# Gate projections as seven half-size products: weight sums on GpSimd, result sums on VectorE

## The reference

```
def trunk_layer(x, ple, pos, lp, lb, cache):
    proj = x @ lp['w_in']
    cq, ckv, kr, f_pre, q_pre, i_pre, g_pre, ga, gb = jnp.split(proj, ...)
    ...
    merged = jax.nn.sigmoid(ga) * (a @ lp['w_br_a']) + jax.nn.sigmoid(gb) * (o @ lp['w_br_b'])
    x = layernorm(DN_ALPHA * x + merged @ lp['w_out'], lp['ln1_g'], lp['ln1_b'])
    moe_out = hier_moe(x, ...)
    ...
```

## Time and profile before

| | us |
|---|---|
| median of 3 runs (lowest, highest) | 1529.96 (1529.62, 1530.68) |
| profiled execution, first to last instruction (span) | 1528.1 |
| PE busy | 1285.5 (84%) |
| PEld busy | 723.5 (47%) |
| DVE busy | 403.9 (26%) |
| ACT busy | 284.9 (19%) |
| POOL busy | 54.0 (4%) |

### The profile page before, as it was taken

The page is one execution under the profiler, slowest core; times in us unless marked ns, Lnnn a source line. Parts: engine busy times, 40 slices in busy tenths (PEclk is TensorE's granted clock), DMA queues, the critical chain, the costliest instruction groups (busy, mean ns, idle before and its releaser), DMA issues.

```text
span 1528.1 us, 20304 instructions
## 1 busy us (share of the span) xinstructions
PE 1285.5 (84%) x8528; PEld 723.5 (47%) x8529; DVE 403.9 (26%) x1027; ACT 284.9 (19%) x712; POOL 54.0 (4%) x94
## 2 busy tenths in 40 slices
PE   6999999999788767767799999999997886667655
PEld 4766887554332322322276678766442332223211
DVE  4142633542111101001133446245311111011003
ACT  2342522021001101000044434212111011010001
POOL 1300000000000000000022010000000000000000
PEclk9999999999898878788899999999998988788778
DMA  9503434999999999999972043579999999999994
GB/s 332 164 1 111 173 117 180 396 367 429 429 431 429 431 429 430 430 429 431 376 245 84 15 149 120 179 249 392 382 430 430 429 432 429 431 427 432 430 425 167
DMA packets 78799, 488.78 MB, mean 320 GB/s; under 512 B 7216, under 2 KB 13296, under 8 KB 49648
## 3 DMA queue, kind: packets, MB, share of 16 engines
q1 hardware_dynamic: 74240, 476.47, 75.9%
q0 software_dynamic: 4464, 10.93, 2.4%
HBM read 484.48 MB, written 2.89 MB: 319 GB/s over the span
## 4 chain that ended last, share of the span: by engine, by line
PE 61%; DMA 34%; DVE 3%; issue 1%; SPq 1%; ACT 0%; POOL 0%; DVEq 0%
PE bank L1036 59%; DMA ring<-in_w_e_down 12%; DMA ring<-in_w_e_up 9%; DMA ring<-in_w_e_gate 5%; DMA arena<-in_w_e_gate 4%; DMA arena<-in_w_e_up 4%; PE bank L1086 2%; DMA ring<-in_w_in 1%; DVE arena L2153 0%; SPq L933 0%; DVE arena L2041 0%; DVE x_sb L2050 0%; ACT xT L1642 0%; DVE small L2490 0%; DVE arena L2073 0%
## 5 line engine op out<-in xcount | busy, mean ns | idle before, releaser
L1036 PE MATMUL bank<-arena 128*32 128x512 f32 (+11 forms) x2808 | 572.3, 541 | 174.5 <-DMA ring<-in_w_e_up 71.0
L1036 PE MATMUL bank<-ring,arena 128*32 128x512 f32 (+4 forms) x1360 | 422.1, 650 | 32.3 <-DMA arena<-in_w_e_gate 15.7
L1036 PEld LDWEIGHTS bank<-arena 128*32 128x32 f32 (+6 forms) x2808 | 211.0, 137 | 441.1 <-issue 436.3
L1036 PE MATMUL bank<-ring,xT 128*32 128x128 f32 (+5 forms) x1536 | 237.5, 364 | 1.4 <-ACT xT L1642 1.1
L1036 PE MATMUL bank<-xT,ring 128*128 128x288 f32 x768 | 191.8, 407 | 0.0
L1036 PEld LDWEIGHTS bank<-ring,xT 128*32 128x32 f32 (+1 forms) x1536 | 121.6, 137 | 100.9 <-issue 90.5
L1036 PEld LDWEIGHTS bank<-ring,arena 128*32 128x32 f32 (+1 forms) x1360 | 108.5, 131 | 121.1 <-issue 114.4
L1036 PEld LDWEIGHTS bank<-xT,ring 128*128 128x128 f32 x768 | 143.7, 190 | 37.9
L1036 PE MATMUL bank<-arena,x_sb 128*128 128x128 f32 (+1 forms) x768 | 99.7, 282 | 1.4 <-DVE arena L2373 0.8
L1036 PEld LDWEIGHTS bank<-arena,x_sb 128*128 128x128 f32 (+1 forms) x768 | 90.5, 190 | 19.4 <-issue 12.7
L1036 PE MATMUL bank<-cst,arena 128*32 128x512 f32 x144 | 90.5, 788 | 0.0
(11 more groups left out here) (232 smaller groups left out, 877.7 us busy)
## 6 DMA issues: line engine op xcount, KB each, us to landing
arena<-in_w_e_up SPq DMA_DIRECT2D x34, 2048.0 KB, 32.1
arena<-in_w_e_gate SPq DMA_DIRECT2D x28, 2048.0 KB, 27.0
ring<-in_w_e_gate SPq DMA_DIRECT2D x24, 2048.0 KB, 25.1
ring<-in_w_e_up SPq DMA_DIRECT2D x20, 2048.0 KB, 24.7
arena<-in_w_e_down SPq DMA_DIRECT2D x20, 2048.0 KB, 22.4
ring<-in_w_e_down SPq DMA_DIRECT2D x18, 2048.0 KB, 25.2
ring<-in_w_in SPq DMA_DIRECT2D x32, 1024.0 KB, 9.4
arena<-in_w_e_gate SPq DMA_DIRECT2D x16, 1024.0 KB, 14.1
```

The source lines that it names most:

```text
L1036: return pe.matmul(out, lhsT, rhs, start=first, stop=last, skip_group_check=True)
```

## The change

Each gate projection is cut into quarters: `xT` into two halves of tokens by two halves of the width, the weights into two halves of the width by two halves of the features. Seven products of quarters, some of them of sums of quarters, give the four quarters of the result in place of eight. A product m of a gate is worked out in two parts p (two tiles of 128 features each, 144 columns of tokens each, four chunks of the width): a job (name, m, p) has 8 matmuls of 144 columns, and 288 columns of its bank are used. `SEVEN` is the order of the products, `SUM_OF` names the four that need a sum of weights.

VectorE makes the five sums of tokens once in a layer, into free parts of `lb` and `lnw`. GpSimd adds weight quarters in the ring's slots in place, four times a gate. ScalarE copies the results of products 4, 5 and 3; VectorE adds each product but 4 into the gates. Each product's bank is emptied by VectorE's last add from it (of product 4: by ScalarE's copy). The order of the pieces and their last uses follow.

```diff
-GATE_AT = {("ss",): [("ga", 0), ("ga", 1)], ("lat",): [("ga", 2)],
-           ("A", 0, 1): [("ga", 3)], ("A", 0, 3): [("ga", 4)], ("ks", 0): [("ga", 5)], ("o", 0): [("ga", 6)],
-           ("A", 1, 1): [("ga", 7)], ("A", 1, 3): [("gb", 0)], ("ks", 1): [("gb", 1)], ("o", 1): [("gb", 2)],
-           ("A", 2, 0): [("gb", 3), ("gb", 4)], ("ks", 2): [("gb", 5)], ("o", 2): [("gb", 6), ("gb", 7)]}
+SEVEN = (4, 5, 3, 2, 7, 1, 6)
+SEVEN_WEIGHTS = {1: (1, 1), 2: (0, 0), 3: (1, 0), 4: (0, 0), 5: (1, 1), 6: (1, 0), 7: (0, 1)}
+SUM_OF = {2: 1, 7: 2, 1: 3, 6: 4}
+
+
+def seven_of(name, *ms):
+
+    return [(name, m, p) for m in ms for p in range(2)]
+
+
+GATE_AT = {("ss",): seven_of("ga", 4, 5), ("lat",): seven_of("ga", 3),
+           ("A", 0, 1): seven_of("ga", 2), ("A", 0, 3): seven_of("ga", 7), ("ks", 0): seven_of("ga", 1), ("o", 0): seven_of("ga", 6),
+           ("A", 1, 1): seven_of("gb", 4), ("A", 1, 3): seven_of("gb", 5), ("ks", 1): seven_of("gb", 3), ("o", 1): seven_of("gb", 2),
+           ("A", 2, 0): seven_of("gb", 7, 1), ("ks", 2): seven_of("gb", 6)}
...
+                def sum_halves(name):
+
+                    ns = {(j, h): piece_number(layer, (name, j, h)) for j in range(2) for h in range(2)}
+                    for n in ns.values():
+                        pool.wait_ge(ring_full[SIGNAL_OF[n]], 16 * FILLS[n])
+                    w = {at: slot(n) for at, n in ns.items()}
+                    job_done(pool, (layer, name, 4, 1))
+                    pool.tensor_tensor(w[0, 0], w[0, 0], w[0, 1], ALU.add).then_inc(half_sums, 1)
+                    pool.wait_ge(half_sums, summed_halves(layer, name, 2))
+                    pool.tensor_tensor(w[0, 1], w[0, 1], w[1, 1], ALU.add).then_inc(half_sums, 1)
+                    pool.wait_ge(half_sums, summed_halves(layer, name, 7))
+                    job_done(pool, (layer, name, 5, 1))
+                    pool.tensor_tensor(w[1, 1], w[0, 0], w[1, 1], ALU.add).then_inc(half_sums, 1)
+                    pool.wait_ge(half_sums, summed_halves(layer, name, 1))
+                    job_done(pool, (layer, name, 3, 1))
+                    pool.tensor_tensor(w[1, 0], w[1, 0], w[1, 1], ALU.add).then_inc(half_sums, 1)
+
+                sum_halves("ga")
                 job_read(pool, (layer, "aTs"))
                 pool.dma_start(state[1][:, :, :], state_hgrn[layer, 0].rearrange("h k v -> k h v")).then_inc(state_in, 16)
+                sum_halves("gb")
...
-                    for name, f in GATE_AT.get(place, []):
-                        by_features(layer, (name, f), f % 4, [(name, f // 4, 0), (name, f // 4, 1)], xT)
+                    for name, m, p in GATE_AT.get(place, []):
+                        n = piece_number(layer, (name,) + SEVEN_WEIGHTS[m])
+                        arrived(n)
+                        pe.wait_ge(forms_out, layer + 1)
+                        if m in SUM_OF:
+                            pe.wait_ge(half_sums, summed_halves(layer, name, m))
+                        w = slot(n).rearrange("p (c n) -> p c n", c=4)
+                        b = open_bank((layer, name, m, p))
+                        for u in range(2):
+                            f = 2 * p + u
+                            for c in range(4):
+                                ins = mm(b[:, S * u:S * u + S], w[:, c, P * f:P * f + P], seven_tokens[m][c], c == 0, c == 3)
+                        done(ins)
...
+                        job_done(dve, key)
+                        if m in (5, 3):
+                            dve.wait_ge(gate_copied, copied_gates(layer, name, m, p))
+                        before = SEVEN[SEVEN.index(m) - 1]
+                        job_read(dve, (layer, name, before, p))
+                        to = {5: [(0, 0, ALU.subtract)], 3: [(0, 1, ALU.add)], 2: [(1, 0, ALU.add), (1, 1, ALU.subtract)],
+                              7: [(0, 0, ALU.add)], 1: [(0, 0, ALU.add), (1, 1, ALU.add)], 6: [(1, 1, ALU.add)]}[m]
+                        for i, j, op in to:
+                            g = seven_gate(name, i, j, p)
+                            ins = dve.tensor_tensor(g, g, seven_bank(key), op)
+                        emptied(ins, key)
...
+                gates_at("ss")
...
                 def place_part(t, j):
 
                     n = NT[t]
+                    gates_at("A", t, j)
...
+                        if t == 0 and k == 3:
+                            gates_at("lat")
...
+                    gates_at("ks", t)
+                    gates_at("o", t)
```

More of the change, by code:

```diff
@@ L143, in weight_pieces @@
     out += [("g", 0), ("g", 1)]
-    for j in range(2):
-        out += [("ga", j, 0), ("ga", j, 1), ("gb", j, 0), ("gb", j, 1)]
+    out += [(name, j, h) for name in ("ga", "gb") for j in range(2) for h in range(2)]
     out += [(w, j) for w in ("bra", "brb") for j in range(2)]
@@ L540, in build, with quarter, tiles, seven_gate @@
         mT = xT
+        S = T // 2
+        def quarter(i, k):
+            return xT[:, 4 * k:4 * k + 4, S * i:S * i + S]
+        def tiles(a):
+            return a.rearrange("p (c t) -> p c t", t=S)
+        xa = tiles(lbr[:, 40:40 + 4 * S])
+        xb = tiles(lbr[:, 40 + 4 * S:40 + 8 * S])
+        xc_parts = [tiles(lbr[:, 40 + 8 * S:40 + 10 * S]), tiles(early[:, 4 * T:4 * T + 2 * S])]
+        xd = tiles(early[:, 4 * T + 2 * S:4 * T + 6 * S])
+        whole = lambda a: [a[:, c, :] for c in range(4)]
+        seven_tokens = {1: whole(xa), 2: whole(quarter(1, 1)), 3: whole(quarter(0, 0)), 4: whole(xb), 5: whole(quarter(0, 1)),
+                        6: [part[:, c, :] for part in xc_parts for c in range(2)], 7: whole(xd)}
+        def seven_gate(name, i, j, p):
+            pair = gate_pair((0 if name == "ga" else FEATURES // 2) + 2 * j + p)
+            return pair.rearrange("p (u t) -> p u t", u=2)[:, :, S * i:S * i + S]
         acc = carve(0, 2, D)
@@ L667, in build @@
         more_read = sem("more_read")
+        forms_out = sem("forms_out")
+        half_sums = sem("half_sums")
+        gate_copied = sem("gate_copied")
         block = ctx.enter_context(nc.Block())
@@ L684, in bank, with seven_bank, summed_halves, copied_gates @@
             return banks[book.bank(key)]
+        def seven_bank(key):
+            return bank(key)[:, 0:T].rearrange("p (u t) -> p u t", u=2)
+        def summed_halves(layer, name, m):
+            return 8 * layer + 4 * (name == "gb") + SUM_OF[m]
+        def copied_gates(layer, name, m, p):
+            return 8 * layer + 4 * (name == "gb") + 2 * (m == 3) + p + 1
         def further_passes(eng, layer, turn, body, each_pass=None):
@@ L1714, in gates_at @@
                 def gates_at(*place):
-                    for name, f in GATE_AT.get(place, []):
-                        key = (layer, name, f)
+                    for name, m, p in GATE_AT.get(place, []):
+                        key = (layer, name, m, p)
+                        if m not in (4, 5, 3):
+                            continue
                         job_done(act, key)
-                        emptied(act.copy(dict(ga=gate_a, gb=gate_b)[name][f], bank(key)[:, 0:T]), key)
+                        if m == 4:
+                            act.copy(seven_gate(name, 0, 0, p), seven_bank(key))
+                            emptied(act.copy(seven_gate(name, 1, 0, p), seven_bank(key)), key)
+                        else:
+                            act.copy(seven_gate(name, 0 if m == 5 else 1, 1, p), seven_bank(key)).then_inc(gate_copied, 1)
                 for h in range(HH):
@@ L1852, in gate_values @@
                     for k in pairs:
-                        for i in (2 * k, 2 * k + 1):
-                            job_read(act, (layer, "ga" if i < FEATURES else "gb", i % FEATURES))
+                        job_read(act, (layer, "ga" if k < 4 else "gb", 6 if k // 2 % 2 else 1, k % 2))
                         act.activation(gate_pair(k), gate_pair(k), ACT.Sigmoid).then_inc(early_gates, 1)
@@ L2101, in _, with gates_at @@
                                                      kn_row[0:n, :], ALU.mult, ALU.mult), key)
+                for t in range(3):
+                    job_read(dve, (layer, "tx", t, 1))
+                dve.tensor_tensor(xc_parts[0], quarter(1, 0)[:, 0:2, :], quarter(0, 0)[:, 0:2, :], ALU.subtract)
+                dve.tensor_tensor(xc_parts[1], quarter(1, 0)[:, 2:4, :], quarter(0, 0)[:, 2:4, :], ALU.subtract)
+                step(dve.tensor_tensor(xb, quarter(1, 0), quarter(1, 1), ALU.subtract))
+                step(dve.tensor_tensor(xa, quarter(0, 0), xb, ALU.subtract))
+                dve.tensor_tensor(xd, quarter(0, 1), xa, ALU.subtract).then_inc(forms_out, 1)
+                def gates_at(*place):
+                    for name, m, p in GATE_AT.get(place, []):
+                        key = (layer, name, m, p)
+                        if m == 4:
+                            continue
+                        job_done(dve, key)
[9 more added lines that the diff above has]
+                        emptied(ins, key)
```

4 lines of the change are left out of this document (3 added, 1 removed).

## The result

The changed kernel takes 1563.4 us (median of 4 runs, 1562.1 to 1563.8) against 1529.8 for the kernel before (4 runs): ratio 1.022, 95% interval 1.0209 to 1.0233. It is slower by 33.6 us. The profiled execution has a span of 1561.8 us, 1.6 under the median.

What follows compares the result with a forecast made beforehand. TensorE bounds the stage up to the first expert load, DMA what follows. Products 55.6 plus waits 7.4 against 62.1 lose 0.9, stopped reads 15.7: 16.6 a layer, 33 for two, 1529.96 + 33 = 1563 us; range 1525 to 1580.

Steps and rivals of the forecast that it cites:

- The stage and the border: Gate stage before the first expert load: its gain or loss moves the end equally; 16.6 us lost a layer, taken twice.
- The products: TensorE's gate products: 448 instructions of 144 columns at 0.124 us, 55.6 against 62.1, 6.5 us saved a layer.
- The bound by the gathers: TensorE's gate products: upper bound of 0.145 us per 144-column instruction, 65.0 us a layer, 2.9 lost.
- VectorE's place in line: Gate products on banks 6 and 7 wait for VectorE's earlier adds: 0.9, 3.2, 2.1 and 1.2, together 7.4 us a layer.
- GpSimd's adds: Eight weight-quarter adds a layer on GpSimd, 128 x 2048, all in SBUF: about 4.5 us each.
- Stopped reads: VectorE's two-input SBUF work stops while GpSimd adds: 15.7 us a layer, time 1563, chance 0.60.
- The first large wait: Tile 0's levels, held by GpSimd, delay ScalarE's read of "lat" to 166.2; TensorE, needing it at 159.1, waits 7.7 us.
- The second: Second gate's product 3, due at 214.8, waits for product 5's add in tile 2's level 4, done 222.8: 8.0 us.
- VectorE runs on, 1532: VectorE unhindered beside GpSimd, but waits for banks 6 and 7 eat the saving: 0.9 us lost a layer, chance 0.17.
- Rival 2: VectorE runs on and reaches the gate banks sooner, waits of 3.5 us a layer left: 1524 us, chance 0.12.
- Rival 3: VectorE runs on, but 144-column instructions cost the gathers' rate, products 65.0 us a layer: 1542 us, chance 0.11.
- The sign of a short add: If GpSimd's add is near 2 us, its holds fit into VectorE's own gaps: some 1534 us, forecast wrong.

Runs made afterwards that it cites:

- the fastest version: Changed kernel with weight sums by DMA, four gate banks, first gate's product 6 and second gate's product 4 swapped: 1515.0 us, ratio 0.9908.
- ScalarE's version: Changed kernel with GpSimd clearing instead of adding, ScalarE copying every product's result and VectorE making no gate adds: 1524.0 us, ratio 0.9965.

## Why the prediction was right, step by step

**The stage and the border.** Right. The stage is 17.05 us longer in the first layer and 17.29 in the second (16.6 forecast), together 34.3; the spans differ by 33.7. The stretches outside the stage nearly cancel: the first expert loads begin 18.25 and 36.23 us later than before, so 1.2 us is lost ahead of the first stage and 0.7 between the stages, and behind the second border 2.5 come back. What these small differences are stays open; the start of the first stage differs by as much among versions that are alike up to it (138.19 to 140.44).

**The products.** Forecast 0.124 an instruction, 6.5 saved a layer. From 170.03 to 173.95 it is 3.92/32 = 0.1225, and the undisturbed stage of the fastest version shows 6.6. The bound by the gathers (0.145) was far off.

**VectorE's place in line.** Forecast waits of 0.9, 3.2, 2.1 and 1.2; measured in the changed kernel 0.63, 3.00, about 0.2 (what is left of the window's idle time when the others are taken off) and 1.09. The 2.1 at ("o", 0) failed for the clock: product 1 in front of it ran 1.74 us longer, at a granted clock of 0.63 (187.80 to 190.50) and 0.75 (190.50 to 193.40), and TensorE came later by that. The second layer bears this out. There product 7 is the long one (5.83), TensorE comes later to product 1, and the four waits are 0.66, 1.32, 1.81 and 1.09.

**GpSimd's adds.** Forecast 4.5, a term that no run of before shows; measured 4.49 to 4.61 in the sixteen rows of the two layers.

**Stopped reads.** Right, and the whole of the loss: without reads 1528.8, with the same sums by DMA 1531.8, with reads 1563.4. That a reading GpSimd instruction holds VectorE until it is over no row of before shows: the memset of the earlier trace rows reads nothing. The choice between the two cases was the author's estimate (0.60). The runs show it. Two-input instructions: 4.38 us for one column beside an add, 1.74 beside a copy, 0.43 for 256 columns beside a clearing; those with one input in PSUM kept their length beside an add (0.81 for two gate adds). The scaling, with one SBUF input of 544 columns, took 4.62 beside an add, 2.00 beside a copy and 1.61 beside a clearing, in place of 0.50.

**The first large wait.** Wrong in place and size. The step said "ScalarE reads "lat" (157.18 before) behind the decays of level 3, at 166.2, so TensorE, which needs it at 159.1, waits 7.7 us". There was no such wait. I had let VectorE enter the levels on time; but the second of the two softmax scalings ahead of them was blocked (4.38 and 4.62), and TensorE stood for 5.70 us ahead of the transposes. Having lost that time there, and 1.8 us more at a granted clock of 0.50 (154.20 to 156.40) and 0.85 (156.40 to 161.00), it came to the projection at 167.96, just as ScalarE had read "lat" (167.34 to 167.91). The forecast time of that read, 166.2, was good: this stage began 1.2 us later than before, at 140.44, which makes it 167.4. It came about in another way, by levels that began 7 us late and met one hold in place of three. What the forecast left out is what VectorE does before the levels. Where the second scaling isn't held for long, the forecast wait does appear: 3.66 us with the adds in pieces, 0.56 in the old kernel with adds beside it.

**The second.** Right. Forecast 8.0 ahead of product 3 of gb, behind level 4; measured 7.76 at this place, for the add that stands behind two holds of 4.56 and 4.41.

**What no step had.** The clock. Waits were forecast at 7.4 + 15.7 = 23.1 a layer and measured at 113.88 − 95.55 = 18.3. Slower work behind three of them makes it up: 2.39 against 1.26 for the transposes (with GpSimd clearing), 4.77, 5.83 and 5.70 against 4.09 for products, 1.13 + 0.68 + 1.74 + 1.61 = 5.2. 18.3 + 5.2 = 23.5, and the undisturbed stage of 90.2 makes 113.7 of the 113.9 measured. So the mechanism was right, but that the total came out to within 1 us is luck: two errors cancel, 4.8 too much idle time and 5.2 of clock forgotten.

**The rivals.** "VectorE runs on, 1532" is about what the kernel does as soon as GpSimd doesn't read (1528.8 to 1531.8); its sum was right for a case that did not hold. Rival 2's 1524 does not come by itself: with two banks nothing went under 1528.8 where VectorE adds. Rival 3's price is excluded by the 0.1225. The sign of a short add, some 1534, is close to what the copies of 1.9 us gave, 1530.6.

## What to carry to other kernels

Before moving elementwise work to an idle GpSimd, look at what VectorE does at that moment: in these runs a VectorE instruction with two SBUF inputs stood beside a reading GpSimd instruction until that was over (4.38 us for one of 0.16), and splitting didn't help here, where the chain on VectorE is dense (1559.9 us against 1563.4). A DMA that adds took the work over without holding VectorE (two-input instructions at 0.42 to 0.43). But its sums came 7.5 to 13.5 us after their issue, so the order of the work had to leave them that time: one late sum held TensorE for 4.87 us.

Work saved on TensorE was worth only as much as the readers of its banks could follow. Here 6.6 us a layer were there all along, and came out only when filler jobs had four banks and every sum was early; removing one wait alone showed the next one.

When you price a wait on TensorE, allow for a low clock behind it. Where that came in these traces (0.50 to 0.75 of full speed in the first 2.5 to 2.7 us), the product of 4.09 us right behind the wait was 1.45 us (5.54, with the adds in pieces) to 2.85 us (6.94, second layer with the DMA sums) longer. The length of the wait alone does not tell whether it comes, as the last section shows.

## What the hardware showed that was not expected

- Alternation: with GpSimd's adds cut to 512 columns, eleven VectorE instructions in a row took 1.37 to 1.50 us (0.42 alone), and sixteen GpSimd adds 21.88 us, 1.37 each.
- A clearing on GpSimd (no read) still held a one-input scaling on VectorE, 1.61 against 0.50 us, and a one-input copy in SBUF, 0.94 against 0.23, but no two-input instruction (0.43).
- A GpSimd copy of 2048 columns takes 1.89 us where the two-input add takes 4.5. Its single read blocked VectorE for 1.74 to 2.00 us.
- In ScalarE's version an idle time of TensorE of 1.94 us was followed by a product of 5.83 (clock 0.57 in the window 203.3 to 206.0), as one of 3.00 was in the changed kernel; one of 1.09 was followed by 4.16. In the version with DMA sums the clock after the 3.00 is 0.59:

```profile
178.50:181.00 2.50, 2.50 (x12) 2.50 (x13) 2.40 (x7) 0.25 (x1) 0.00 (x0) 0.59 1.01 217
```

- The idle time right ahead of a product does not decide this alone. In the first layer of the changed kernel 0.63 us was followed by a product of 4.16; in the second, at the same place of the order, 0.66 was followed by 5.83, with clock 0.54 from 946.1 to 948.6, and then 1.32 by 4.16. What makes the difference, no run here shows.

```profile
946.07 5.83 PE L1105 MATMUL bank<-lnw,ring 128*128 128x144 f32 x32 [0.66 <-DVE arena L2210]
```
